# A block inverse by doubling, rewritten to accumulate in PSUM with one burst a level, inside a two-layer RWKV-7 and attention trunk

## The reference

```python
sa = jnp.einsum('bhij,bhj->bhi', state, a_t)
state = (state * w_t[:, :, None, :] + sa[..., None] * b_t[:, :, None, :]
         + v_t[..., None] * k_t[:, :, None, :])
return state, jnp.einsum('bhij,bhj->bhi', state, r_t)
```

## Time and profile before

| what | value |
|---|---|
| times of three runs | 2741.64, 2743.44, 2744.86 us (median 2743.44) |
| span of the profiled execution, first to last instruction | 2739.9 us |
| the profiled execution's own time | not listed apart; it lies among the three above, 1.7 to 5.0 us over its span |
| busy: PE, DVE, ACT, POOL | 97%, 63%, 45%, 9% of the span |
| mean granted TensorE clock | 0.995 of full speed |
| mixer passes | 16, of 64.7 us from one to the next |

### The profile page before, as it was taken

How to read it: one execution, slowest core, us unless ns; L and a number is a source line. 1 busy time by engine, 2 the same in 40 slices (tenths; PEclk the granted TensorE clock), 3 DMA queues, 4 the chain that set the end, 5 groups by cost and what they waited for, 6 DMA issues and landing times.

```text
span 2739.9 us, 50433 instructions
## 1 busy us (share of the span) xinstructions
PE 2669.7 (97%) x16843; PEld 2188.6 (80%) x16843; DVE 1729.0 (63%) x2858; ACT 1220.3 (45%) x1976; POOL 239.9 (9%) x341
## 2 busy tenths in 40 slices
PE   7999999999999999999899999999999999999998
PEld 6777777777888888888777777777778888888886
DVE  5766666656656656556567667666566565565665
ACT  5444444445434444444454444444454344344443
POOL 4111111100000000000022222221000000000000
PEclk9999999999999999999999999999999999999999
DMA  6333333355556555565533333333455655655554
GB/s 202 95 108 103 100 96 101 102 165 168 187 198 188 190 182 188 199 188 187 180 106 108 101 102 97 99 102 100 169 171 187 195 177 199 191 184 193 183 193 152
DMA packets 438043, 420.25 MB, mean 153 GB/s; under 512 B 19518, under 2 KB 351952, under 8 KB 437968
## 3 DMA queue, kind: packets, MB, share of 16 engines
q1 hardware_dynamic: 434320, 412.75, 48.1%
q0 software_dynamic: 3648, 6.52, 0.9%
HBM read 417.10 MB, written 2.10 MB: 153 GB/s over the span
## 4 chain that ended last, share of the span: by engine, by line
PE 91%; DVE 5%; issue 1%; ACT 1%; DMA 0%; DVEq 0%; SPq 0%; POOL 0%; ACTq 0%; POOLq 0%
PE gemm_bank L516 28%; PE gemm_bank L517 15%; PE gemm_bank L541 11%; PE gemm_bank L543 11%; PE gemm_bank L542 10%; PE gemm_bank L519 2%; PE mix_bank L698 2%; PE mix_bank L710 1%; PE mix_bank L707 1%; PE mix_bank L662 1%; DVE b_rn L1267 1%; PE mix_bank L728 1%; PE mix_bank L732 1%; PE mix_bank L742 1%; PE mix_bank L738 1%
## 5 line engine op out<-in xcount | busy, mean ns | idle before, releaser
L516 PE MATMUL gemm_bank<-b_hT,b_whi 128*128 128x512 f32 x3420 | 1267.0, 409 | 2.2 <-DVE b_zt L1162 2.2
L1156 DVE TENSOR_TENSOR b_wlo<-b_raw,b_whi 128x1024 fp32r<-128x1024 f32 x745 | 907.0, 1229 | 524.3 <-ACT b_whi L890 521.7
L890 ACT ACTIVATE b_whi<-b_raw 128x1024 fp32r<-128x1024 f32 x777 | 810.2, 1057 | 610.8 <-PE gemm_bank L543 421.2
L517 PE MATMUL gemm_bank<-b_hT,b_wlo 128*128 128x256 f32 x3648 | 1014.0, 282 | 0.0
L516 PEld LDWEIGHTS gemm_bank<-b_hT,b_whi 128*128 128x128 f32 x3420 | 643.4, 188 | 168.4 <-issue 22.4
L517 PEld LDWEIGHTS gemm_bank<-b_hT,b_wlo 128*128 128x128 f32 x3648 | 690.9, 189 | 14.8 <-issue 5.3
L541 PE MATMUL gemm_bank<-b_whi,b_mT 128*128 128x512 f32 x1280 | 502.9, 393 | 0.0
L543 PE MATMUL gemm_bank<-b_whi,b_mT 128*128 128x512 f32 x1280 | 498.4, 389 | 0.0
L542 PE MATMUL gemm_bank<-b_wlo,b_mT 128*128 128x512 f32 x1280 | 498.2, 389 | 0.0
L541 PEld LDWEIGHTS gemm_bank<-b_whi,b_mT 128*128 128x128 f32 x1280 | 240.3, 188 | 51.1 <-issue 1.7
L543 PEld LDWEIGHTS gemm_bank<-b_whi,b_mT 128*128 128x128 f32 x1280 | 240.3, 188 | 50.2
(11 more groups left out here) (242 smaller groups left out, 2287.0 us busy)
## 6 DMA issues: line engine op xcount, KB each, us to landing
b_raw<-in_w_up SPq DMA_DIRECT2D x256, 512.0 KB
b_raw<-in_w_down SPq DMA_DIRECT2D x256, 512.0 KB
b_raw<-in_w_in SPq DMA_DIRECT2D x384, 256.0 KB
b_raw<-in_w_out SPq DMA_DIRECT2D x60, 512.0 KB
b_raw<-in_w_in SPq DMA_DIRECT2D x8, 512.0 KB
b_xt<-in_x SPq DMA_DIRECT2D x4, 512.0 KB, 6.0
b_raw<-in_w_out SPq DMA_DIRECT2D x8, 256.0 KB
out<-b_xt SPq DMA_DIRECT2D x8, 256.0 KB, 2.4
```

Of the source, the lines that this page charges most:

```text
L516: mm(bank[b0 + b][:, :], whi[r][:, cols], pair, start=first, stop=False)
L517: m = mm(bank[b0 + b][:, 0:SEQ], wlo[r][:, cols], act[:, kt, 0, :], start=False, stop=False)
L890: f(whi[r][:, :], raw[r][:, :, :].rearrange("p a b -> p (a b)"), ACT.Copy).then_inc(hi_done, 1)
L1156: tt(wlo[r][:, :], flat(raw[r][:, :, :]), whi[r][:, :].bitcast(F32), ALU.subtract).then_inc(lo_done, 1)
```

## The change

T and its transpose Y are no longer copied block by block. Each has its own place in PSUM, into which every level adds. N is computed untransposed by eight matmuls that also open the banks of N T; T starts as N's transpose, by eight matmuls against the identity. At each level DVE takes X as the masked part of the bank of N T (one operation for each w, all six masks in the form 64 x 64), ACT copies the running Y out beside it, and one burst of PE adds both to N T and to T. At the end DVE adds the identity. The four transposes, the eight identity copies on POOL and all predicated copies go. One tick is left behind each of levels 1 to 4, none behind levels 0 and 5. The others stand behind the last matmul of the chunks, between there and the end of the pass: ticks are 7, 4, 3, 2, 3, then four of 1, nine of 1 in the chunks, then 3, 2, 3, 2, 2 and the remaining 4 (before: 7, 4, 2, 2, 2, twelve of 1, nine of 1, then 2, 2 and the remaining 6). Scores, mask and maxima go behind the chunks, the rope's products partly into chunk 1, and steps 3 to 7 of the weights and both finishes are placed anew.

```diff
@@ constants: identity of 64 columns added, masks now 64 x 64 for each level @@
+    levels = np.zeros((P, LEVELS, CHUNK), np.float32)
...
@@ POOL @@
-                for a in range(4):
-                    for b in range(2):
-                        nc.gpsimd.tensor_copy(TT[:, a, b, :], ident).then_inc(e["tt_reset"], 1)
@@ PE @@
-                fill(2)
+                fill(3)
...
-                    fill(2)
+                    fill(3 if u else 2)
                 pe.wait_ge(e["gram_ready"], 4 * n + 4)
-                for unit in range(4):
-                    m = turned(mb[2][:, P * unit:P * unit + P], G[:, unit, 2, :], ident)
-                m.then_inc(e["n_turned"], 1)
-                fill(1)
...
+                for u in range(2):
+                    for j in range(2):
+                        for h in range(2):
+                            hs = slice(HEAD * h, HEAD * h + HEAD)
+                            m = mm(y_cols(h, u)[halves[j ^ h], :], AR[hs, u, 0, halves[j ^ h]],
+                                   btl[hs, u, halves[j ^ h]], start=u == 0, stop=False, skip_group_check=True)
+                m.then_inc(e["n_sum"], 1)
+                for w in range(2):
+                    if w:
+                        wait_alone(pe, e["akv_out"], V)
+                    for u in range(2):
+                        for half in halves:
+                            mm(mb[w][half, CHUNK * u:CHUNK * u + CHUNK], ident[half, half], G[half, 2 * w + u, 2, half],
+                               start=u == 0, stop=False, skip_group_check=True)
+                for lv in range(LEVELS):
                     for w in range(2):
+                        wait_alone(pe, e["x_ready"], 2 * LEVELS * n + 2 * lv + w + 1)
+                        if lv:
+                            wait_alone(pe, e["yt_ready"], 2 * (LEVELS - 1) * n + 2 * lv + w - 1)
+                        for u in range(2):
+                            unit = 2 * w + u
+                            old = (lambda half: YT[half, unit, :]) if lv else (lambda half: G[half, unit, 2, half])
                             if lv < LEVELS - 1:
                                 for half in halves:
+                                    mm(blocks(y_cols(w, u)[half, :], lv, 0), old(half),
+                                       blocks(X[half, unit, :], lv, 0), start=False, stop=False, skip_group_check=True)
                             for half in halves:
+                                m = mm(mb[w][half, CHUNK * u:CHUNK * u + CHUNK], X[half, unit, :], old(half),
+                                       start=False, stop=lv == LEVELS - 1, skip_group_check=True)
+                        m.then_inc(e["lev_sum"], 1)
+                    if 0 < lv < LEVELS - 1:
+                        fill(1)
+                wait_alone(pe, e["tt_ready"], 2 * n + 2)
...
-                    if c == 0:
-                        pe.wait_ge(e["roped"], V)
...
+                    if 0 < c < NCH - 1:
                         fill(1)
+                fill(3)
+                pe.wait_ge(e["roped"], V)
+                mm(mb[1][:, 0:P], qr[:, 0, 0:P], qr[:, 1, 0:P], start=True, stop=True)
+                mm(mb[1][:, P:3 * P], qr[:, 0, P:2 * P], qr[:, 1, :], start=True,
+                   stop=True).then_inc(e["score_sum"], 1)
+                fill(2)
                 pe.wait_ge(e["masked"], V)
...
                 if more:
                     key_norms(n + 1)
+                fill(3)
                 pe.wait_ge(e["probs"], V)
@@ ACT: finish(0) now ahead of akv_out; Y copied at levels 1 to 5 @@
+                        act.wait_ge(e["lev_sum"], 2 * LEVELS * n + 2 * lv - 1 + w)
+                        f(YT[:, 2 * w:2 * w + 2, :], mb[w][:, 0:P].rearrange("p (a b) -> p a b", a=2),
+                          ACT.Copy).then_inc(e["yt_ready"], 1)
...
@@ ACT chunks: c 0 swapped; c 1 step 4; c 2 step 5; c 3 step 6, finish 1, step 7, exponentials @@
@@ DVE @@
+                for lv in range(LEVELS):
+                    for w in range(2):
+                        if lv:
+                            dve.wait_ge(e["lev_sum"], 2 * LEVELS * n + 2 * lv - 1 + w)
+                        tt(X[:, 2 * w:2 * w + 2, :], mb[2 + w][:, 0:P].rearrange("p (a b) -> p a b", a=2),
+                           lvl[:, lv, :].unsqueeze(1).to_broadcast([P, 2, CHUNK]), ALU.mult).then_inc(e["x_ready"], 1)
+                    if lv == 3:
+                        step(3)
+                    if lv:
+                        gap[lv]()
+                for w in range(2):
+                    dve.wait_ge(e["lev_sum"], 2 * LEVELS * n + 2 * LEVELS - 1 + w)
+                    tt(TT[:, 2 * w:2 * w + 2, :], mb[w][:, 0:P].rearrange("p (a b) -> p a b", a=2),
+                       cst[:, C_ID2:C_ID2 + CHUNK].unsqueeze(1).to_broadcast([P, 2, CHUNK]),
+                       ALU.add).then_inc(e["tt_ready"], 1)
...
@@ DVE: gap is finish(0), bonus gate, norm gate, cosine products 0 and 1 at levels 1 to 5; chunk 1 sine product and rope add; chunk 2 step 4 @@
+                step(5)
+                finish(1)
+                step(6)
+                dve.wait_ge(e["score_sum"], V)
+                tt(sm[:, :], mb[1][:, 0:384], cst[:, C_CAUS:C_CAUS + 384], ALU.add).then_inc(e["masked"], 1)
...
                 if more:
                     key_norms(l, i + 1, n + 1)
+                step(7)
```

More of the change, by code:

```diff
@@ L690, in mixer @@
-                for lv in range(1, LEVELS):
-                    for w in range(2):
-                        if lv == 1 and w == 0:
-                            wait_alone(pe, e["akv_out"], V)
-                        wait_alone(pe, e["level_done"], 2 * LEVELS * n + (2 if lv == 1 else 2 * lv - 1 + w))
-                        for unit in (2 * w, 2 * w + 1):
-                            for half in halves:
-                                m = mm(packed(mb[2 + w][half, narrow(unit, half)], lv), G[half, unit, 2, half],
-                                       blocks(TT[half, unit, 0, half], lv, 0), start=True, stop=True)
-                        m.then_inc(e["x_sum"], 1)
-                    fill(1)
-                    for w in range(2):
-                        wait_alone(pe, e["x_out"], 2 * (LEVELS - 1) * n + 2 * lv - 1 + w)
-                        for unit in (2 * w, 2 * w + 1):
+                for u in range(2):
[4 more added lines that the diff above has]
+                                   btl[hs, u, halves[j ^ h]], start=u == 0, stop=False, skip_group_check=True)
@@ L1022, in mixer @@
                     if c == 0:
+                        act.wait_ge(tile_out, tiles + 2)
+                        for a, b in ((0, 64), (64, 0)):
+                            f(xs[a:a + 64, :, :], zt[b:b + 64, 3:5, 1:SEQ + 1], ACT.Copy).then_inc(e["swapped"], 1)
+                    if c == 1:
+                        step(4)
+                    if c == 2:
+                        step(5)
+                    if c == 3:
+                        step(6)
+                        finish(1)
                         step(7)
-                    if c == 2:
-                        finish(1)
-                    if c == 3:
                         act.wait_ge(e["nmax"], V)
@@ L1398, in mixer @@
                             dve.wait_ge(e["s_out"], (NCH - 1) * n + c + 1)
+                step(5)
+                finish(1)
+                step(6)
+                dve.wait_ge(e["score_sum"], V)
+                tt(sm[:, :], mb[1][:, 0:384], cst[:, C_CAUS:C_CAUS + 384], ALU.add).then_inc(e["masked"], 1)
+                dve.wait_ge(e["masked"], V)
+                nc.vector.tensor_reduce(small[:, 8:9], sm[:, 0:P], AX.X, ALU.max)
+                nc.vector.tensor_reduce(small[:, 9:10], sm[:, P:3 * P], AX.X, ALU.max).then_inc(e["smax"], 1)
+                dve.wait_ge(e["smax"], V)
+                ts(small[:, 10:12], small[:, 8:10], -SCALE, None, ALU.mult).then_inc(e["nmax"], 1)
                 if more:
                     key_norms(l, i + 1, n + 1)
+                step(7)
                 dve.wait_ge(e["expd"], 2 * n + 2)
```

156 lines of the change are left out of this document (46 added, 110 removed).

## The result

| what | before | after |
|---|---|---|
| median (lowest to highest), same chip | 2744.15 (2741.64 to 2745.95), 4 runs | **2814.68** (2803.17 to 2842.33), 4 runs |
| ratio, 95% interval | | **1.0271** [1.0219, 1.0323], slower |
| profiled execution: span | 2739.9 | 2801.5 (own time 2803.17) |
| mean granted TensorE clock, four runs | 0.995 (profiled execution) | 0.977, 0.970, 0.974, 0.962 |

A forecast was written before the change was run, and what follows sets the result against it. TensorE, busy 97% of the 2739.9 us span, bounds the kernel. Layer 1 +8.8, layer 0 +3.7 and last passes -0.7 make +11.8, on the 2743.4 median 2755 us; own range 2748 to 2765, overall 2739 to 2774.

The forecast's parts named there:

- three signs that the prediction named for being wrong: No PE wait at the key norms; level steps not near 1.95; layer 1 passes at most as long as before.
- Part 1, levels: Line 676 to chunk 0: 11.74 us with its ticks, 8.94 without, against 11.29 before; 2.35 saved a pass.
- rival 3: Levels: costlier handover, masked copies of 0.50 and waits before bursts, 1.35 a pass, 22 us, 2777; chance 0.09.
- Rival 4: Levels: 64-wide matmuls run one after another, so no saving, 2.8 a pass more, 2800; chance 0.03.
- Part 2, chunks: Scores leave chunk 0, which gets no shorter; PE idles 0.90 there; no weight transfer is waited for.
- Part 3, behind the chunks: Ticks, scores, key norms: PE idles 1.2, scores to probability transposes 6.3, line 764 to those transposes +7.8.
- Rival 1: Key norms: DVE reaches them before PE, saving 1.2 in each of 14 passes, 2738 (2734 to 2742); chance 0.2.
- Part 4, the tail: Behind P: line 641 stays at P + 15.44 in layer 1; PE waits 0.65 for slot 12's split.
- Part 5, POOL's copies: Without POOL's eight copies line 641 comes 0.84 sooner in layer 0, passes 1 to 6; nothing in layer 1.

The follow-up runs named there:

- e10: The changed kernel plus two unread 256-column products at the end of chunk 0, ahead of the wait for the state: 2763.35, ratio 1.0070.
- e2: The changed kernel plus three unread 256-column products, one behind level 5 and two at the end of chunk 0, no tick moved: 2766.01, ratio 1.0088.
- e11: The kernel before, old levels, with both ticks of level 5 and the tick of chunk 0 moved ahead of the levels: 2763.69, ratio 1.0049.
- e5: The change with two ticks moved late (to behind level 5 and chunk 0's end; 2744.70), plus key-norm product behind the next three ticks: 2734.69, ratio 0.9976.
- e6: The change with two ticks moved late (to behind level 5 and chunk 0's end; 2744.70), plus POOL's eight copies back, unread: 2749.46, ratio 1.0029.
- e7: The kernel before, old levels, with the second tick of level 5 and chunk 0's tick moved ahead of the levels: 2741.66, ratio 1.0001.
- e9: The changed kernel plus one unread 256-column product behind level 5, ahead of the wait for T: 2781.41, ratio 1.0123.

## Why the prediction missed

**What failed is the sum's silent term.** "Levels, chunks, tail" were priced at the durations of a kernel whose passes all ran at full clock, and no rival had the clock in it. I read the mean clock, 0.995, and not that it hung on PE's work staying dense. The price is 41 of the 61.6 us in the profiled execution (clock 0.977); the slower executions have lower clocks (2842.33 at 0.962), though their falls aren't traced. With the clock kept up and nothing else changed but two unread products, e10 gives 2763.35, which lies in the range; 18.6 over its before, for a forecast of 11.8. None of the three signs that the prediction named for being wrong came: PE waits at the key norms, the levels take 2.01 for 1.95, and the passes are longer. The miss lay where no sign pointed.

The prediction named both idle places (0.55 for T, 0.90 for the state) and priced each by its length. Each was nearly right: 0.49 and 0.83. What they cost beyond that was the clock of the 10.2 to 20.5 us behind them, in six of the 16 passes. The Trainium skill, page "TensorE: Matmul & The Clock Gate", section "A second HAM failure mode: psum-queue depth-cycling", says of another kernel that frequent short idling between groups of matmuls made the clock swing between its two levels. This trace and e2, e10 and e11 agree. The same page of the Trainium skill, section "HAM oscillation — how this bites in real kernels", tells of falls through long waits for a transfer; here no wait from level 5 to a fall is longer than 0.93, and none is for a transfer.

**Part 1, levels: mis-sized by 0.78.** Forecast 11.74, measured 12.52. Level 0 starts at 1.89 (1.88 forecast). Level 0 to 1 takes 1.41, not 1.03: 0.26 of idle stands there, at the one step between levels where no tick covers the exchange with DVE and ACT. Levels 1 to 4 are 8.05, not 7.80; from level 5 to chunk 0 it is 1.17, not 1.03. The masked copy is 0.29, as taken, so rival 3's price was wrong in its cause, but part of its sum was there. Rival 4 would have added 2.8; level 5, eight 64-wide matmuls, takes 0.68 without its wait (1.17 less 0.49) for a forecast of 0.64 to the end of its second half, so it is out.

**Part 2, chunks: right.** The idle time in chunk 0 was 0.83 for a forecast of 0.90. PE waited for no weight transfer; ACT's waits for them were 7.5 in all, against 22.8 before.

**Part 3, behind the chunks: right.** S to P 6.29 for 6.3, key norms 1.24 for 1.2. Rival 1 (DVE reaches them in time) didn't come. e5 shows that the wait was on the path, worth 0.73 to 0.80 a pass.

**Part 4, the tail: right in time, wrong in one wait.** P to line 637 is 15.45 for 15.44, since DVE's chain hangs on POOL's splits and these start 7.76 behind P. The wait at line 637 is 0.67 in layer 1 and 1.0 to 1.2 in layer 0 (less in the first pass of each), not 1.4 to 1.5. That figure didn't follow from the prediction's own terms: in layer 1, where PE hadn't waited, the next pass starting at P + 7.6 instead of 8.35 makes 0.75.

**Part 5, POOL's copies: borne out, but not by its own test.** In layer 0 line 637 stands 346.10 - 330.59 = 15.51 behind P; 16.47 before, so 0.96 sooner for a forecast of 0.84, and layer 0 is 1.03 shorter than layer 1 (forecast 0.9). By the rule of the Trainium skill, page "SBUF — State Buffer", section "SBUF: two separate sides", the prediction had worked out 0.1, which would have left the layers nearly alike; the measured 0.96 speaks against it. e6 didn't bring the delay back, so that the copies alone were its cause stays argued.

**The undisturbed passes.** 65.77 for 65.1 and 66.80 for 66.0: the misses of 0.67 and 0.80 are Part 1's 0.78. Over 16 passes they are 12 us, 2767 instead of 2755, still inside the range.

**What stays open.** Why one pass falls and the next, with the same instructions, doesn't; what sets how long a fall lasts; and whether e7 is safe or was only not seen to fall.

## What to carry to other kernels

When a change takes filler work away from PE, price a stretch that becomes thin not only by its waits but by whether the granted clock survives it, and read that clock by stretches before and after. Even products that nobody reads, put at the last wait ahead of the fall, show in one run whether that is the cause. Price a tick by where it stands: here it costs 0.70 beside other ticks, 0.9 to 1.1 between small matmuls. Judge a new algorithm and the order that comes with it apart: here the new inverse in the old order gains 1.5%, and in its own order it loses 2.7%.

## What was not expected of the hardware

- The clock fell to 1.2 GHz in a kernel whose PE is busy 96% of the span, behind idle times of 0.48 and 0.83 with one tick between them.
- With the same instructions ahead of it and behind it, a fall lasted 10.2, 17.1 or 20.5 us in one execution of the change, or didn't come; in e9 each of three lasted 27.3.
- With one tick less in the old kernel's level 5, and on another chip, the spread over the runs was 81 us (e11) instead of 3 (e7).
- Beside eight 128-column copies on POOL back to back, one DVE operation took 0.84 longer; beside the same eight with waits between them 0.07 at most.
